# Gated-delta inverse: the transposed factor of the next level by TensorE transposes in place of a second product

## Chip, cores and metric

One core of one Trainium2 chip runs the whole program in one launch. The metric is the device time of one execution in microseconds (us). Names of engines here and in the profile: TensorE is PE (its weight loads PEld), VectorE is DVE, ScalarE is ACT, GpSimd is POOL, SyncE is SP.

## What is computed

The reference is a stack of transformer blocks on 256 tokens of width 1024, in fp32: four blocks of feed-forward, mixer, feed-forward (mixers: gated delta, stick-breaking, sparse attention, gated delta), then a second stack of two blocks. The change lies in the gated-delta mixer (eight heads of 128, chunks of 64 tokens), in the solution of a triangular system for each head and chunk:

```
lower = jnp.where(strict, beta[..., :, None] * kk * decay, 0.0)
eye = jnp.eye(c, dtype=jnp.float32)
rhs = jnp.concatenate([v * beta[..., None], k * (beta * jnp.exp(g_cum))[..., None]], axis=-1)
sol = lax.linalg.triangular_solve(lower + eye, rhs, left_side=True, lower=True, unit_diagonal=True)
```

## The kernel before, in words

The kernel works with tiles of 128 tokens in place of chunks of 64 and inverts the unit triangular matrix itself. A mixer handles its heads in two halves of four heads; with two token tiles each, a half inverts eight 128x128 matrices at once. They form two groups of four, A and B, and a group fills one bank of PSUM (`wrk`, four banks, 128x512 fp32 each).

`invert(half)` doubles the size of the inverted diagonal blocks in six levels (`LEVELS`, block sizes 2 to 64). V is the inverse so far, kept in `g_vi`, and U its transpose, kept in `g_u`; both are parts of `arena`. GpSimd multiplies the transposed matrix with the mask of a level into `g_lts` (two buffers, L2366). For each group a level does:

- X = product of `g_lts` and `g_vi` on TensorE (L848), which ScalarE copies from PSUM to `g_xs` (`copy_out`, the helper at L1124);
- Y = product of `g_u` and `g_xs`, and YT = product of `g_xs` and `g_u` (both L856); VectorE subtracts Y from `g_vi` and YT from `g_u` (both L1949). The last level needs only U, so it makes only YT.

Ahead of level 0 the eight matrices U are transposed on TensorE to give V (L840). Behind the last level `states` multiplies with U (`u0`, L865).

The order is written out by hand. Each engine runs its own program, and semaphores join them: `filled` counts the PSUM banks that TensorE has filled, `taken` those that have been read out. The list `gdn_uses` gives the order in which banks are used, and `taken` rises in that order only: a reader waits, beside its bank, until all uses ahead of it in the list have been taken (`frees`), and TensorE fills a bank only when the use four places back has been taken (`bank`). `held(label)` makes TensorE wait until that use has been taken, since its next product reads what the taker wrote.

After each level VectorE and ScalarE do a job that has nothing to do with the inversion (`jobs(lv)`). In the first half VectorE's are the taps of the convolution at levels 0 to 2 (`taps`, six instructions, L1849), then the low part of a weight piece at levels 3 and 4 (`w_lo`, L1633, 128x2048). In the second half they are weight pieces at levels 0, 1 and 4, and at levels 2 and 3 the gated output of a pair of heads (L1984) and its low part `h_lo` (L1645), which waits for ScalarE's `h_hi` of the same pair; ScalarE makes that in its own job one level later, behind its copies of X. ScalarE's other jobs are weight pieces (`w_hi`), silu and table loads.

Weight pieces of 1 MB come by SyncE's queue into three slots (`raw`); ScalarE makes `w_hi` and VectorE `w_lo` of them, and TensorE multiplies with both.

Of the kernel before, what the change touches and what calls it, by code (L numbers as in the profile page):

```python
# [14 lines left out]
P = 128  # L15
T = 256
# [11 lines left out]
LEVELS = [2, 4, 8, 16, 32, 64]  # L28
# [72 lines left out]
def gdn_uses():  # L101
    u = ["gates", "cols"]
    for half in range(2):
        u += [f"D{half}{p}" for p in range(2)] + [f"ss{half}{p}" for p in range(4)]
        for n in ("kk", "B", "kq"):
            u += [f"{n}{half}{p}" for p in range(2)]
        u += [f"tr{half}{p}" for p in range(3)]
        u += [f"vt{half}{g}" for g in "AB"]
        for lv in range(len(LEVELS)):
            u += [f"X{half}{lv}{g}" for g in "AB"]  # L110
            for g in "AB":
                u += ([f"Y{half}{lv}{g}"] if lv < len(LEVELS) - 1 else []) + [f"YT{half}{lv}{g}"]
        u += [f"u0_{half}", f"S_{half}", f"R_{half}", f"u1_{half}"]
        u += [f"o{half}0", f"o{half}1", f"os{half}0", f"os{half}1"]
    return u
# [153 lines left out]
def build(nc, wts, vec_d, const_d, x_d, c_d, bias_d, mods_d, rows_d, out, ops):  # L269
    starts, use, total = schedule(ops)  # L270

    with ExitStack() as ctx:
# [36 lines left out]
        def cst(name, a=0, b=None):  # L309
            at, w = CONST[name]  # L310
            return const[:, at + a:at + (w if b is None else b)]
# [56 lines left out]
        filled = sem("filled")  # L368
# [160 lines left out]
        def _(pe):  # L529
# [225 lines left out]
            def gdn(i, name, prm):  # L755
# [77 lines left out]
                def invert(half):  # L833

                    k = 2 * g + half
                    pe.wait_ge(stage("gdn_u1"), k + 1)
                    for a, grp in enumerate("AB"):
                        o = put(f"vt{half}{grp}")
                        for b in range(4):
                            m = tr(o[:, b * P:(b + 1) * P], g_u[:, 4 * a + b, :], cst("ident"))  # L840
                        m.then_inc(filled, 1)
                    for lv in range(nl):
                        pe.wait_ge(stage("gdn_lts"), nl * k + lv + 1)
                        for a, grp in enumerate("AB"):
                            o = put(f"X{half}{lv}{grp}")
                            held(f"vt{half}{grp}" if lv == 0 else f"YT{half}{lv - 1}{grp}")
                            for b in range(4):
                                m = mm(o[:, b * P:(b + 1) * P], g_lts[:, lv % 2, 4 * a + b, :], g_vi[:, 4 * a + b, :], start=True, stop=True)  # L848
                            m.then_inc(filled, 1)
                        for a, grp in enumerate("AB"):  # L850
                            held(f"X{half}{lv}{grp}")
                            for label, lh, rh in (("Y", g_u, g_xs), ("YT", g_xs, g_u)):
                                if label == "YT" or lv < nl - 1:
                                    o = put(f"{label}{half}{lv}{grp}")
                                    for b in range(4):
                                        m = mm(o[:, b * P:(b + 1) * P], lh[:, 4 * a + b, :], rh[:, 4 * a + b, :], start=True, stop=True)  # L856
                                    m.then_inc(filled, 1)

                def states(half, between):

                    k, heads = 2 * g + half, range(half * HALF, half * HALF + HALF)
                    held(f"YT{half}{nl - 1}B")
                    o = put(f"u0_{half}")
                    for b in range(HALF):
                        m = mm(o[:, b * P:(b + 1) * P], g_u[:, 2 * b, :], g_bv[:, 2 * b, :], start=True, stop=True)  # L865
                    m.then_inc(filled, 1)
                    between(0)
                    held(f"u0_{half}")
                    o = put(f"S_{half}")
                    for b in range(HALF):  # L870
                        m = mm(o[:, b * P:(b + 1) * P], g_kd[:, b, :], g_u0[:, b, :], start=True, stop=True)
                    m.then_inc(filled, 1)
                    between(1)
                    held(f"S_{half}")
                    o = put(f"R_{half}")
                    for b in range(HALF):
                        m = mm(o[:, b * P:(b + 1) * P], g_k[:, heads[b], P:T], g_s[:, b, :], start=True, stop=True)
                    m.then_inc(filled, 1)
                    between(2)
                    held(f"R_{half}")  # L880
                    o = put(f"u1_{half}")
                    for b in range(HALF):
                        m = mm(o[:, b * P:(b + 1) * P], g_u[:, 2 * b + 1, :], g_bv[:, 2 * b + 1, :], start=True, stop=True)
                    m.then_inc(filled, 1)
                    between(3)
                    held(f"u1_{half}")
                    for j in range(2):
                        o = put(f"o{half}{j}")
                        for b in (2 * j, 2 * j + 1):
                            w = (b % 2) * T  # L890
                            mm(o[:, w:w + P], g_u0[:, b, :], g_qk[:, b, 0:P], start=True, stop=True)
                            mm(o[:, w + P:w + T], g_s[:, b, :], g_q[:, heads[b], P:T], start=True, stop=False)
                            m = mm(o[:, w + P:w + T], g_vi[:, b, :], g_qk[:, b, P:T], start=False, stop=True)
                        m.then_inc(filled, 1)
                    between(4)
                    for j in range(2):
                        pe.wait_ge(stage("gdn_osq"), 2 * k + j + 1)
                        mm(put(f"os{half}{j}"), cst("ones"), g_lts[:, j, 0:4, :].rearrange("p a b -> p (a b)"), start=True, stop=True).then_inc(filled, 1)
                    between(5)
# [726 lines left out]
        def _(dve):  # L1626
# [186 lines left out]
            def gdn(i, name, prm):  # L1813
# [4 lines left out]
                def frees(label):  # L1818
                    dve.wait_ge(taken, use[name, label])
# [119 lines left out]
                def invert(half, jobs):  # L1939

                    for lv in range(len(LEVELS)):
                        for a, grp in enumerate("AB"):
                            for label, t in (("Y", g_vi), ("YT", g_u)):
                                if label == "YT" or lv < len(LEVELS) - 1:
                                    l_ = f"{label}{half}{lv}{grp}"
                                    full(l_)
                                    frees(l_)
                                    v = flat(t[:, 4 * a:4 * a + 4, :])
                                    tt(v, v, bk(l_), ALU.subtract).then_inc(taken, 1)  # L1949
                        jobs(lv)  # L1950

# [681 lines left out]
```

## Time and profile before

| | |
|---|---|
| Median of 3 executions | 3757.82 us (3750.78 to 3761.15) |
| The profiled execution | 3753.37 us |
| Its span in the profile | 3751.3 us |
| PE busy | 3521.9 us, 94% |
| DVE busy | 2192.3 us, 58% |
| ACT busy | 1872.8 us, 50% |
| POOL busy | 583.7 us, 16% |
| Mean granted TensorE clock | 0.971 of full |
| HBM over the span | 173 GB/s |

The profile is one execution. Busy shares are averages over stages with different limits; what counts here is what each engine does within the four inversions, which begin at 326.80, 418.60, 2047.20 and 2138.99 us of the span. An idle time in a row is that of its engine just ahead of the row, with what ended it. A product of two fp32 tiles of 128x128 shows as two rows of TensorE, a transpose as one. A timeline merges rows of one kind that follow each other; a merged row's length runs to the end of its last one, which overlaps the next by the depth of the pipeline. PEclk is the granted clock as a share of 2.4 GHz. A row of windows gives a stretch's start and end, its length, the busy time and instructions of PE, PEld, DVE, ACT and POOL in this order, then PEclk, the busy share of the DMA engines and GB/s.

### The profile page before, as it was taken

What the parts mean: (1) busy time and instruction counts of PE and PEld (TensorE: products, weight loads), DVE (VectorE), ACT (ScalarE), POOL (GpSimd) and SP (SyncE); (2) the same over time, 40 slices, a digit from 0 to 9 for tenths busy, and PEclk for the clock granted to TensorE, in tenths of its full rate; (3) what the DMA queues carried; (4) which work ended last, traced back from release to release, by engine and by line L of the source; (5) the groups of instructions that cost most, each with busy time, mean ns of one, the idle gap of its engine ahead of it and who ended that gap; (6) DMA issues with size and microseconds to landing.
All of it is one profiled execution on the core that took longest, in us unless ns stands there. A gap on an engine that the chain in (4) does not pass through costs nothing. (4 is left out here: it accounts for less than half of the span.)

```text
span 3751.3 us, 44766 instructions
## 1 busy us (share of the span) xinstructions
PE 3521.9 (94%) x18374; PEld 2981.0 (79%) x18374; DVE 2192.3 (58%) x2284; ACT 1872.8 (50%) x2398; POOL 583.7 (16%) x208
## 2 busy tenths in 40 slices
PE   7999899999899997799999999999999799999999
PEld 6889778888788876688878878888888478788887
DVE  4666566665666666666567555555555544545554
ACT  4664356664456562456564444555443344544443
POOL 1511115240134330143421100000000000000000
PEclk9999899999999998899999899999999899999999
DMA  6642156564376753376753135555554125454453
GB/s 247 226 156 78 47 191 224 216 229 161 112 270 241 274 204 122 124 258 254 257 185 112 58 134 190 180 185 185 180 181 165 37 92 187 170 176 160 169 202 129
DMA packets 89975, 653.54 MB, mean 174 GB/s; under 512 B 10032, under 2 KB 10032, under 8 KB 10928
## 3 DMA queue, kind: packets, MB, share of 16 engines
q1 hardware_dynamic: 78768, 573.10, 42.2%
q0 software_dynamic: 11008, 77.60, 5.8%
q8 instruction: 148, 2.42, 0.3%
q14 instruction: 51, 0.42, 0.0%
HBM read 649.61 MB, written 1.05 MB: 173 GB/s over the span
## 5 line engine op out<-in xcount | busy, mean ns | idle before, releaser
L1633 DVE TENSOR_TENSOR w_lo<-raw,w_hi 128x2048 fp32r<-128x2048 f32 x540 | 1391.2, 2581 | 684.2 <-ACT w_hi L1124 684.1
L1124 ACT ACTIVATE w_hi<-raw 128x2048 fp32r<-128x2048 f32 x540 | 1030.3, 1912 | 550.3 <-PE acc L540 376.5
L538 PE MATMUL wrk<-w_hi,h_hi 128*128 128x512 f32 (+1 forms) x2496 | 967.6, 388 | 35.2 <-DVE w_lo L1633 23.2
L540 PE MATMUL wrk<-w_hi,h_lo 128*128 128x512 f32 (+1 forms) x2496 | 952.4, 382 | 0.0
L539 PE MATMUL wrk<-w_lo,h_hi 128*128 128x512 f32 (+1 forms) x2496 | 950.9, 381 | 0.0
L538 PEld LDWEIGHTS wrk<-w_hi,h_hi 128*128 128x128 f32 x2496 | 470.6, 189 | 125.8 <-DVE w_lo L1633 29.6
L2389 POOL TENSOR_TENSOR arena<-arena,c 128x2048 f32<-128x2048 f32 x92 | 467.2, 5082 | 562.1 <-ACT arena L1124 531.5
L540 PEld LDWEIGHTS wrk<-w_hi,h_lo 128*128 128x128 f32 x2496 | 470.4, 188 | 92.0
L539 PEld LDWEIGHTS wrk<-w_lo,h_hi 128*128 128x128 f32 x2496 | 471.0, 189 | 84.5 <-issue 0.2
L538 PE MATMUL acc<-w_hi,hid_hi 128*128 128x512 f32 x1144 | 448.1, 392 | 2.9 <-DVE hid_lo L1713 2.8
L540 PE MATMUL acc<-w_hi,hid_lo 128*128 128x512 f32 x1144 | 445.4, 389 | 0.0
L539 PE MATMUL acc<-w_lo,hid_hi 128*128 128x512 f32 x1144 | 445.1, 389 | 0.0
L1124 ACT ACTIVATE hid_hi<-wrk 128x512 fp32r<-128x512 f32 x143 | 85.5, 598 | 466.8 <-PE wrk L635 466.8
L1124 ACT ACTIVATE arena<-wrk 128x256 f32<-128x256 f32 (+2 forms) x261 | 127.0, 488 | 300.7 <-PE wrk L540 170.6
L538 PEld LDWEIGHTS acc<-w_hi,hid_hi 128*128 128x128 f32 x1144 | 214.7, 188 | 49.1 <-issue 5.7
L540 PEld LDWEIGHTS acc<-w_hi,hid_lo 128*128 128x128 f32 x1144 | 214.7, 188 | 45.1
L539 PEld LDWEIGHTS acc<-w_lo,hid_hi 128*128 128x128 f32 x1144 | 214.9, 188 | 43.7
L1124 ACT ACTIVATE arena<-arena 128x1024 f32<-128x1024 f32 (+2 forms) x238 | 231.5, 979 | 26.8 <-DVE arena L2058 17.5
L538 PE MATMUL wrk<-h_hi,w_hi 128*128 128x256 f32 x660 | 194.6, 295 | 24.7 <-DVE h_lo L1664 14.6
L1713 DVE TENSOR_TENSOR hid_lo<-wrk,hid_hi 128x512 fp32r<-128x512 f32 x143 | 98.3, 687 | 204.0 <-ACT hid_hi L1124 204.0
L539 PE MATMUL wrk<-h_lo,w_hi 128*128 128x256 f32 x660 | 192.7, 292 | 0.0
L540 PE MATMUL wrk<-h_hi,w_lo 128*128 128x256 f32 x660 | 192.4, 292 | 0.0
(267 smaller groups left out, 3887.1 us busy)
## 6 DMA issues: line engine op xcount, KB each, us to landing
raw<-in_wts SPq DMA_DIRECT2D x540, 1024.0 KB, 4.8
arena<-in_mods POOLq DMA_DIRECT2D x72, 1024.0 KB, 5.2
const<-in_const SPq DMA_DIRECT2D x1, 2176.0 KB, 10.2
c<-in_bias POOLq DMA_DIRECT2D x8, 256.0 KB, 3.0
x<-in_x SPq DMA_DIRECT2D x1, 1024.0 KB, 5.3
c<-in_c SPq DMA_DIRECT2D x1, 1024.0 KB, 5.0
out<-x SPq DMA_DIRECT2D x1, 1024.0 KB, 3.9
row<-in_rows SPq DMA_DIRECT2D x1, 512.0 KB, 11.5
```

Of the source, the lines that this page charges most:

```text
L538: nc.tensor.matmul(o, l_h, r_h, start=first, stop=False, skip_group_check=True)
L539: nc.tensor.matmul(o, l_h, r_l, start=False, stop=False, skip_group_check=True)
L540: return nc.tensor.matmul(o, l_l, r_h, start=False, stop=last, skip_group_check=True)
L1124: return nc.scalar.activation(o, i, f, **kw)
L1633: tt(w_lo[:, ns % SLOTS, :], raw[:, ns % SLOTS, :], w_hi[:, ns % SLOTS, :].bitcast(F32), ALU.subtract).then_inc(lo_ready, 1)
L1713: tt(hid_lo[:, s % 2, :, :], wrk[:, use[name, f"t{s}"] % BANKS, :].rearrange("p (a b) -> p a b", b=T), hid_hi[:, s % 2, :, :].bitcast(F32) ...
L2389: nc.gpsimd.tensor_tensor(halves(m_prod[:, g % 2, :]), halves(m_raw[:, m % 2, :]), m_rows[:, w, :].unsqueeze(1).to_broadcast([P, 2, D]), A ...
```

## The change

`YT` as a second product at levels 0 to 4 is gone. In its place TensorE transposes V at the start of the next level (`T`, levels 1 to 5), and VectorE copies the result over U. At level 0 U is still the matrix that V was transposed from. The order of bank uses in a level is now X of A and B, T of A and B, Y of A and B; the last level makes its product with the operands swapped and subtracts it from U, as YT did. `Y` waits for both the X and the T of its group.

```diff
--- before.py
+++ after.py
@@ -107,9 +107,8 @@
         u += [f"tr{half}{p}" for p in range(3)]
         u += [f"vt{half}{g}" for g in "AB"]
         for lv in range(len(LEVELS)):
-            u += [f"X{half}{lv}{g}" for g in "AB"]
-            for g in "AB":
-                u += ([f"Y{half}{lv}{g}"] if lv < len(LEVELS) - 1 else []) + [f"YT{half}{lv}{g}"]
+            for n in ("X", "T", "Y"):
+                u += [f"{n}{half}{lv}{g}" for g in "AB" if n != "T" or lv]
         u += [f"u0_{half}", f"S_{half}", f"R_{half}", f"u1_{half}"]
         u += [f"o{half}0", f"o{half}1", f"os{half}0", f"os{half}1"]
     return u
@@ -843,23 +842,30 @@
                         pe.wait_ge(stage("gdn_lts"), nl * k + lv + 1)
                         for a, grp in enumerate("AB"):
                             o = put(f"X{half}{lv}{grp}")
-                            held(f"vt{half}{grp}" if lv == 0 else f"YT{half}{lv - 1}{grp}")
+                            held(f"Y{half}{lv - 1}{grp}" if lv else f"vt{half}{grp}")
                             for b in range(4):
                                 m = mm(o[:, b * P:(b + 1) * P], g_lts[:, lv % 2, 4 * a + b, :], g_vi[:, 4 * a + b, :], start=True, stop=True)
                             m.then_inc(filled, 1)
+                        if lv:
+                            for a, grp in enumerate("AB"):
+                                o = put(f"T{half}{lv}{grp}")
+                                for b in range(4):
+                                    m = tr(o[:, b * P:(b + 1) * P], g_vi[:, 4 * a + b, :], cst("ident"))
+                                m.then_inc(filled, 1)
                         for a, grp in enumerate("AB"):
                             held(f"X{half}{lv}{grp}")
-                            for label, lh, rh in (("Y", g_u, g_xs), ("YT", g_xs, g_u)):
-                                if label == "YT" or lv < nl - 1:
-                                    o = put(f"{label}{half}{lv}{grp}")
-                                    for b in range(4):
-                                        m = mm(o[:, b * P:(b + 1) * P], lh[:, 4 * a + b, :], rh[:, 4 * a + b, :], start=True, stop=True)
-                                    m.then_inc(filled, 1)
+                            o = put(f"Y{half}{lv}{grp}")
+                            if lv:
+                                held(f"T{half}{lv}{grp}")
+                            lh, rh = (g_u, g_xs) if lv < nl - 1 else (g_xs, g_u)
+                            for b in range(4):
+                                m = mm(o[:, b * P:(b + 1) * P], lh[:, 4 * a + b, :], rh[:, 4 * a + b, :], start=True, stop=True)
+                            m.then_inc(filled, 1)
 
                 def states(half, between):
 
                     k, heads = 2 * g + half, range(half * HALF, half * HALF + HALF)
-                    held(f"YT{half}{nl - 1}B")
+                    held(f"Y{half}{nl - 1}B")
                     o = put(f"u0_{half}")
                     for b in range(HALF):
                         m = mm(o[:, b * P:(b + 1) * P], g_u[:, 2 * b, :], g_bv[:, 2 * b, :], start=True, stop=True)
@@ -1939,13 +1945,16 @@
                 def invert(half, jobs):
 
                     for lv in range(len(LEVELS)):
-                        for a, grp in enumerate("AB"):
-                            for label, t in (("Y", g_vi), ("YT", g_u)):
-                                if label == "YT" or lv < len(LEVELS) - 1:
-                                    l_ = f"{label}{half}{lv}{grp}"
-                                    full(l_)
-                                    frees(l_)
-                                    v = flat(t[:, 4 * a:4 * a + 4, :])
+                        last = lv == len(LEVELS) - 1
+                        for n in ("T", "Y") if lv else ("Y",):
+                            for a, grp in enumerate("AB"):
+                                l_ = f"{n}{half}{lv}{grp}"
+                                full(l_)
+                                frees(l_)
+                                v = flat((g_u if n == "T" or last else g_vi)[:, 4 * a:4 * a + 4, :])
+                                if n == "T":
+                                    nc.vector.tensor_copy(v, bk(l_)).then_inc(taken, 1)
+                                else:
                                     tt(v, v, bk(l_), ALU.subtract).then_inc(taken, 1)
                         jobs(lv)
```

TensorE's program from the transposes ahead of level 0 to the product behind the last level, first half of a mixer, before (L848 is X, L856 is Y and YT, L865 is u0, counts are products; levels 2 to 4 repeat level 1):

```order
L840 MATMUL wrk<-const,arena 128x128 x8
L848 MATMUL wrk<-arena 128x128 x8
L856 MATMUL wrk<-arena 128x128 x16
L848 MATMUL wrk<-arena 128x128 x8
L856 MATMUL wrk<-arena 128x128 x16
...
L848 MATMUL wrk<-arena 128x128 x8
L856 MATMUL wrk<-arena 128x128 x8
L865 MATMUL wrk<-arena 128x128 x4
```

The same place after the change (L847 is X, L853 the transposes T, L862 is Y, L871 is u0; levels 2 to 4 repeat level 1):

```order
L839 MATMUL wrk<-const,arena 128x128 x8
L847 MATMUL wrk<-arena 128x128 x8
L862 MATMUL wrk<-arena 128x128 x8
L847 MATMUL wrk<-arena 128x128 x8
L853 MATMUL wrk<-const,arena 128x128 x8
L862 MATMUL wrk<-arena 128x128 x8
...
L847 MATMUL wrk<-arena 128x128 x8
L853 MATMUL wrk<-const,arena 128x128 x8
L862 MATMUL wrk<-arena 128x128 x8
L871 MATMUL wrk<-arena 128x128 x4
```

Between X and Y there are now eight transposes from level 1 on, eight products follow where sixteen did, and the last level has a row more.

VectorE's program in the first half, levels 0 to 1, before (L1949 are the takes, L1849 the taps of the job):

```order
L1949 TENSOR_TENSOR arena<-arena,wrk 128x512 x4
L1849 SCALAR_TENSOR_TENSOR arena<-acc,vec,arena 128x255 x2
L1849 SCALAR_TENSOR_TENSOR arena<-acc,vec,arena 128x254 x2
L1849 SCALAR_TENSOR_TENSOR arena<-acc,vec,arena 128x253 x2
L1949 TENSOR_TENSOR arena<-arena,wrk 128x512 x4
L1849 SCALAR_TENSOR_TENSOR c<-acc,vec,c 128x255 x2
L1849 SCALAR_TENSOR_TENSOR c<-acc,vec,c 128x254 x2
L1849 SCALAR_TENSOR_TENSOR c<-acc,vec,c 128x253 x2
```

and after the change (L1956 the copies of T, L1958 the subtractions, L1855 the taps):

```order
L1958 TENSOR_TENSOR arena<-arena,wrk 128x512 x2
L1855 SCALAR_TENSOR_TENSOR arena<-acc,vec,arena 128x255 x2
L1855 SCALAR_TENSOR_TENSOR arena<-acc,vec,arena 128x254 x2
L1855 SCALAR_TENSOR_TENSOR arena<-acc,vec,arena 128x253 x2
L1956 COPY arena<-wrk 128x512 x2
L1958 TENSOR_TENSOR arena<-arena,wrk 128x512 x2
L1855 SCALAR_TENSOR_TENSOR c<-acc,vec,c 128x255 x2
L1855 SCALAR_TENSOR_TENSOR c<-acc,vec,c 128x254 x2
L1855 SCALAR_TENSOR_TENSOR c<-acc,vec,c 128x253 x2
```

Level 0 has two takes in place of four; from level 1 on two copies stand ahead of two subtractions, and the job comes behind all four as it did.

## Rows read from the trace of the kernel before

**Rows 1.** Windows over the two inversions of the first mixer.
```profile
326.80:359.38 32.58, 31.80 (x272) 30.90 (x272) 26.81 (x42) 18.25 (x21) 9.52 (x4) 1.00 0.12 35
418.60:455.52 36.92, 34.27 (x272) 33.18 (x273) 26.00 (x33) 14.64 (x21) 13.14 (x5) 0.94 0.19 61
```

**Rows 2.** TensorE timeline, first half: start us, length us, work, [idle before <- releaser].
```profile
326.80 2.02 PE L848 MATMUL wrk<-arena 128*128 128x128 f32 x16 [0.64 <-ACT arena L1124]
...
328.66 3.79 PE L856 MATMUL wrk<-arena 128*128 128x128 f32 x32
...
332.29 2.17 PE L848 MATMUL wrk<-arena 128*128 128x128 f32 x16
...
337.87 2.17 PE L848 MATMUL wrk<-arena 128*128 128x128 f32 x16
...
354.59 2.17 PE L848 MATMUL wrk<-arena 128*128 128x128 f32 x16
...
359.38 1.16 PE L865 MATMUL wrk<-arena 128*128 128x128 f32 x8 [0.78 <-DVE arena L1949]
```

**Rows 3.** VectorE timeline, first half.
```profile
329.81 0.69 DVE L1949 TENSOR_TENSOR arena<-arena,wrk 128x512 f32<-128x512 f32 x1 [8.20 <-PE wrk L856]
...
332.49 0.69 DVE L1949 TENSOR_TENSOR arena<-arena,wrk 128x512 f32<-128x512 f32 x1 [0.21 <-PE wrk L856]
...
333.09 2.68 DVE L1849 SCALAR_TENSOR_TENSOR arena<-acc,vec,arena 128x255 f32<-128x255 f32 x6
...
335.69 3.07 DVE L1949 TENSOR_TENSOR arena<-arena,wrk 128x512 f32<-128x512 f32 x4
...
355.40 2.28 DVE L1633 TENSOR_TENSOR w_lo<-raw,w_hi 128x2048 fp32r<-128x2048 f32 x1
```

**Rows 4.** ScalarE timeline, first half: copy of X, group A, level 2.
```profile
338.96 0.60 ACT L1124 ACTIVATE arena<-wrk 128x512 f32<-128x512 f32 x1 [2.07 <-PE wrk L848]
```

**Rows 5.** TensorE timeline: the eight transposes before the first half's level 0.
```profile
325.13 1.03 PE L840 MATMUL wrk<-const,arena 128*128 128x128 f32 x8
```

**Rows 6.** Instructions of L1968: engine, form, count: shortest/median/longest ns.
```profile
L1968 DVE COPY c<-wrk x8: 690/692/692, 376.1 to 2188.9; 128x512 f32<-128x512 f32 x8
```

**Rows 7.** TensorE timeline, second half.
```profile
418.60 3.78 PE L848 MATMUL wrk<-arena 128*128 128x128 f32 x16 [0.71 <-POOL arena L2366]
...
422.17 4.28 PE L856 MATMUL wrk<-arena 128*128 128x128 f32 x32
...
437.44 2.16 PE L848 MATMUL wrk<-arena 128*128 128x128 f32 x16
...
444.20 1.13 PE L848 MATMUL wrk<-arena 128*128 128x128 f32 x8 [1.03 <-DVE arena L1949]
...
445.79 1.13 PE L848 MATMUL wrk<-arena 128*128 128x128 f32 x8 [0.45 <-DVE arena L1949]
...
450.32 1.06 PE L848 MATMUL wrk<-arena 128*128 128x128 f32 x8
...
455.52 1.16 PE L865 MATMUL wrk<-arena 128*128 128x128 f32 x8 [0.78 <-DVE arena L1949]
```

**Rows 8.** VectorE timeline, second half.
```profile
423.81 0.69 DVE L1949 TENSOR_TENSOR arena<-arena,wrk 128x512 f32<-128x512 f32 x1 [7.70 <-PE wrk L856]
...
440.57 2.10 DVE L1645 TENSOR_TENSOR h_lo<-h,h_hi 128x256 fp32r<-128x256 f32 x2 [1.45 <-ACT h_hi L1124]
...
442.59 3.04 DVE L1949 TENSOR_TENSOR arena<-arena,wrk 128x512 f32<-128x512 f32 x4
...
447.88 0.76 DVE L1645 TENSOR_TENSOR h_lo<-h,h_hi 128x256 fp32r<-128x256 f32 x2 [1.45 <-ACT h_hi L1124]
```

**Rows 9.** Windows over two stretches of the stick-breaking mixer, columns as in rows 1.
```profile
972.90:986.50 13.60, 7.93 (x42) 6.36 (x41) 9.44 (x22) 6.99 (x17) 0.00 (x0) 1.00 0.00 1
986.50:993.30 6.80, 5.68 (x15) 4.43 (x15) 3.11 (x8) 1.48 (x4) 0.00 (x0) 0.50 0.00 0
```

**Rows 10.** GpSimd timeline, first half.
```profile
328.90 2.38 POOL L2366 TENSOR_TENSOR arena<-arena,const 128x1024 f32<-128x1024 f32 x1 [2.46 <-PE wrk L848]
```

## The prediction

> **What bounds the kernel now.** I read the windows over the four inversions first, then each engine's timeline inside them. In the window of an inversion TensorE's records cover 31.80 of 32.58 us in the first half of a mixer and 34.27 of 36.92 in the second, so TensorE looks like the limit [rows 1]. There are four inversions: two gated-delta mixers, two halves each; the second mixer's windows (2047.20 and 2138.99) are as long as the first's. Together they are 139 us of the 3751.3 us span; nothing else is edited.
>
> The timeline of TensorE shows the period. Levels begin at 326.80, 332.29 and 337.87, and the last at 354.59 [rows 2]: levels 1 to 4 take 22.30 / 4 = 5.58 us each. A level is 48 rows (each fp32 product of 128x128 shows as two rows): 16 of X (L848), 32 of Y and YT (L856). From 328.66 to 332.29 there are 32 rows, 3.63 us, 0.112 per row beside a slower first one, so 48 rows are 5.4 us; the other 0.2 us is group B of X waiting for the last subtraction. VectorE is nearly as full: four subtractions and a job of six tap instructions follow each other without a gap, 333.09 to 335.69 and 3.07 us on [rows 3]. So two engines bind at once, and removing TensorE work is worth only what the second one and the chain between them leave.
>
> The chain has these hops. From the first row of a group of eight to the start of its reader: 337.87 to 338.96, 1.09 us, on ScalarE [rows 2, 4]; 328.66 to 329.81, 1.15 us, on VectorE [rows 2, 3]. From the end of a VectorE take to TensorE's next row: four takes end at 442.59 + 3.04 = 445.63 and TensorE resumes at 445.79, 0.16 us [rows 7, 8]. Takes that wait for each other start 0.79 us apart (3.04 to 3.07 for four, 0.69 each); an unrelated job starts 0.60 us after the last take (332.49 to 333.09) [rows 3].
>
> **What the change removes and adds.** Per inversion the second product (YT) goes from levels 0 to 4: 40 products, 80 rows. The last level keeps the one product per head that it had, and levels 1 to 5 get eight transposes each, 40 rows. A transpose is one row: eight at L840 take 1.03 us with the last row's own length of about 0.27 in it, so 0.109 apiece [rows 5]. Counted: before 96 + 88 x 2 = 272 rows, which is the count in the window [rows 1]; after 96 + 96 + 40 = 232. Forty rows less at 0.112 is 4.5 us per inversion, 18 us in all. That is the most the change can give, reached if no new wait appears.
>
> VectorE's work hardly changes: a level keeps four takes, two being copies instead of subtractions. The nearest row for such a copy is COPY c<-wrk of 128x512, 0.69 us, the same as a subtraction (0.69) [rows 3, 6]. Level 0 has two takes fewer, the last level two more. ScalarE and GpSimd issue what they did; no DMA moves, and each queue past the takes (pieces to split, taps) follows the same level as before.
>
> What changes is the order of waiting. Before, both products of a level start from X, and the next X may start while the YT subtraction runs. Now one level is a serial loop: X, ScalarE's copies of X, the copy of T (which the order of takes puts behind both X copies), Y, subtraction, next X.
>
> **Cost level by level** (first half, full clock). I count from the start of the first T copy. It ends at 0.69; Y of group A starts at 0.85, its subtraction at 2.0 (hop 1.15), that of B 0.90 later at 2.9; VectorE's job starts at 3.5.
> - Levels 1 to 3, job of taps 2.60 (333.09 to 335.69 [rows 3]): the next T copy starts at 6.05 to 6.10. I take 6.05 against 5.58: +0.47 each, +1.4.
> - Level 4, job one weight piece, 2.28 [rows 3]: 5.7 against 5.58, +0.1. Without any job the other loop closes at: X of B at 0.90, its copy at 1.98 to 2.58, T copy 2.68 to 3.37, Y at 3.53, subtraction 4.64 to 5.33, X at 5.5. So even an idle VectorE gives no gain.
> - Level 0: two X groups 1.86 (326.80 to 328.66), 1.15 to the subtraction, 0.69, 0.16: 3.9 against 5.49 [rows 2]: -1.6. This is the one real saving.
> - Last level: T copy at 2.8, Y of A at 3.65, Y of B at 4.54, its subtraction 5.65 to 6.34, next stage at 6.5. Before it is 354.59 to 359.38, 4.79 [rows 2]: +1.7.
>
> First half: -1.6 + 1.4 + 0.1 + 1.7 = **+1.6**.
>
> Second half. Level 0 starts at half clock (418.60 to 422.17 for 16 rows, 0.22 per row [rows 7]); the subtraction comes at 423.81 [rows 8], X again 0.69 + 0.16 later: 6.1 against 7.69 (level 3 starts at 437.44, two levels of 5.58 earlier level 1 at 426.29), -1.6. Levels 1 and 2 carry a weight piece: +0.1 each. At level 3 VectorE is blocked in its job till 442.59, 5.15 into the level: its h_lo waits for ScalarE's h_hi and stands beside GpSimd's multiply [rows 7, 8]. Before, two subtractions then release X (444.20, 6.76). Now copy 0.69, hop 0.16, Y and hop 1.11, subtraction 0.69, hop 0.16 give about 7.9: +1.1. Level 4 the same way: h_lo ends at 448.64 [rows 8], 2.85 after group B of X at 445.79, which now starts 0.9 into the level; VectorE is free at 3.7, the same 2.8 follow, 6.5 against 6.12: +0.4. Last level 6.5 against 5.20: +1.3. Sum **+1.4**.
>
> All: 2 x (1.6 + 1.4) = **+6 us**. Nothing behind gives it back: the stage after an inversion starts with the product that waits for its last take (359.38, 0.78 idle before it [rows 2]), and TensorE is the busy engine from there on. The hops are the soft spot: like ones differ by 0.06 among themselves (1.09, 1.15) and a level has four, so 0.2 us per level, over 22 levels 4.4 us either way.
>
> Against which time: the profiled execution took 3753.37, the median of the three others is 3757.82, and they spread over 10.4 us (3750.78 to 3761.15). The middle of all four is 3755.6; with +6 I say **3761.6**. A difference under 0.3%, 11.3 us, is what a measurement of this kernel cannot tell from none; +6 lies inside.
>
> **A rule against the change.** The granted clock is 1.00 in the first half's inversion and 0.94 in the second's, which begins at the lower level [rows 1, 7]. In the new loop with taps X and T fill the first 2.7 us of a level and Y begins at about 4.05, so TensorE stands still for 1.4 us of each 6.05, beside 0.87 of transposes. In the trace a thinner feed, 7.93 busy of 13.60 us, ran at 1.00, though the clock was 0.50 right after it [rows 9]. So I expect the clock to stay.
> The Trainium skill, in "TensorE: Matmul & The Clock Gate", Part 4 (PE-mode transpose), says that transposes do not count as activity of TensorE in the way products do; by that rule the transposes would be as good as idle and the clock could fall in every inversion. The trace does not decide it: no stretch before alternates products and transposes like this.
>
> **The rivals.**
> - *Slower, by the clock.* If TensorE falls to 1.2 GHz once in each inversion for 6.8 us (the length of 986.5 to 993.3, a stretch at 0.50 [rows 9]), each fall costs about 3: four falls add 12, +18 in all, 3773. If it stays low throughout, each level is some 2 us longer (groups of eight rows 1.7 instead of 0.9 [rows 7], part of it beside VectorE), +45, 3800. It decides from two inversions on. For it: the idle time; against: the 7.93 of 13.60. Chance 0.06.
> - *Slower, by the copies.* h_lo took 2.10 us for two when GpSimd multiplied, 0.76 when it did not [rows 8]. GpSimd's multiply starts when X of B is full, and the T copies fall into it at levels 1 to 3. If they stretch by 1.3 us as h_lo did, it is 12 x 1.3 = 16 more, +22, 3777. Against: the subtraction at 329.81 took its 0.69 beside the multiply of 328.90 to 331.28 [rows 3, 10]; like the copy it reads PSUM. Chance 0.05.
> - *Faster, TensorE alone binds.* If the takes come earlier than I count and only rows matter, -18, 3738. For it: the busy share in the windows [rows 1]. Against: the taps fill VectorE. It needs over 11 of the 18 us; chance 0.04.
> - *The loop is as I say, the hops are shorter or the last level cheaper*: 0 to +3, 3756 to 3759, inside no change.
>
> **How the numbers follow.** The forecast with its short-hop variant has 0.85, all of it within 0.3% but for a tail: +6 with 4.4 of hops and some 5 us of spread between executions passes +11.3 in perhaps one case in sixteen. That gives faster 0.04, same 0.81, slower 0.15. The range takes 4.4 and 5 us plus about 4 for where the runs lie downwards, 3748, and reaches up to the cheaper of the slower rivals, 3776.
>
> **What would show it.** In the changed profile: levels of the first half 6.05 us at levels 1 to 3, 5.7 at level 4, 3.9 at level 0, 6.5 at the last; window of a first half 34.2 us, of a second 38.3; 232 TensorE rows in each; TensorE idle about 1.4 us before L862 in each level, released by the COPY at L1956; that COPY 0.69 us also beside GpSimd; granted clock 1.00 in the first halves. Wrong it would be with the level at 5.0 us or less, the copy well below 0.69, or half clock inside an inversion.

## The result and the profile after

| | before | after |
|---|---|---|
| Median of 20 executions each | 3751.28 us (3747.40 to 3761.15) | 3757.05 us (3752.51 to 3765.83) |
| The profiled execution, its span | 3753.37, 3751.3 us | 3761.97, 3760.2 us |
| PE busy | 3521.9 us, 94% | 3509.9 us, 93% |
| DVE, ACT, POOL busy | 2192.3, 1872.8, 583.7 us | 2191.5, 1876.6, 586.7 us |
| Mean granted clock | 0.971 | 0.971 |

The ratio after to before is 1.0016, with a 95% interval of 1.0009 to 1.0022: 6.0 us slower on 3751.28 (the medians differ by 5.8), and less than the 0.3% that the prediction set as its bound of no change. TensorE has 12 us less to do and the kernel is a little longer. The ratios here and below leave out two executions that ran slow, one of e11 (8734 us at a granted clock of 0.401) and one of the kernel before beside it (4036 us at 0.835).

The windows of the changed kernel, columns as in [rows 1]: first inversion, the stage between, second inversion, for mixer 1 and then mixer 2.

```profile
328.61:362.93 34.32, 28.36 (x233) 26.44 (x233) 26.69 (x42) 18.53 (x21) 9.47 (x4) 1.00 0.16 56
362.93:421.37 58.44, 51.19 (x329) 44.91 (x329) 25.12 (x43) 22.02 (x29) 2.40 (x2) 0.89 0.12 41
421.37:461.06 39.69, 31.59 (x232) 29.79 (x232) 25.84 (x33) 14.83 (x22) 13.10 (x5) 0.91 0.22 74
2050.63:2084.94 34.31, 28.36 (x232) 26.43 (x232) 26.70 (x42) 18.53 (x21) 9.48 (x4) 1.00 0.17 54
2084.94:2144.17 59.23, 52.02 (x328) 45.74 (x329) 25.12 (x43) 22.20 (x29) 2.41 (x2) 0.87 0.11 41
2144.17:2182.51 38.34, 30.63 (x232) 28.70 (x232) 25.75 (x33) 14.66 (x21) 13.10 (x5) 0.94 0.23 77
```

The three stretches of mixer 2 before, and the stage of mixer 1:

```profile
359.38:418.60 59.22, 52.12 (x329) 45.84 (x329) 25.11 (x43) 22.42 (x30) 2.42 (x2) 0.87 0.14 53
...
2047.20:2079.78 32.58, 31.80 (x272) 30.91 (x273) 26.82 (x42) 18.25 (x21) 9.51 (x4) 1.00 0.11 36
2079.78:2138.99 59.21, 52.13 (x328) 45.85 (x328) 25.11 (x43) 22.42 (x30) 2.41 (x2) 0.87 0.15 53
2138.99:2175.88 36.89, 34.25 (x273) 33.15 (x273) 25.98 (x33) 14.64 (x21) 13.14 (x5) 0.94 0.19 61
```

The four inversions took 138.97 us before and take 146.66 after, 7.7 more. TensorE has 232 rows in each where it had 272, and is busy 28.36 of 34.32 us where it was busy 31.80 of 32.58: the rows that went became idle time. The stages between a mixer's two inversions are together 0.8 us shorter. The spans of the two profiles differ by 8.9 us, so 2.0 lie in neither.

TensorE's timeline in the first half, levels 0 to 2 and the end, answers to [rows 2]:

```profile
328.61 2.02 PE L847 MATMUL wrk<-arena 128*128 128x128 f32 x16 [0.64 <-ACT arena L1130]
330.47 2.01 PE L862 MATMUL wrk<-arena 128*128 128x128 f32 x16
332.46 2.02 PE L847 MATMUL wrk<-arena 128*128 128x128 f32 x16
334.32 1.04 PE L853 MATMUL wrk<-const,arena 128*128 128x128 f32 x8
336.55 2.02 PE L862 MATMUL wrk<-arena 128*128 128x128 f32 x16 [1.19 <-DVE arena L1956]
338.55 2.02 PE L847 MATMUL wrk<-arena 128*128 128x128 f32 x16
...
354.43 2.02 PE L862 MATMUL wrk<-arena 128*128 128x128 f32 x16 [0.80 <-DVE arena L1956]
356.43 2.02 PE L847 MATMUL wrk<-arena 128*128 128x128 f32 x16
...
360.12 2.02 PE L862 MATMUL wrk<-arena 128*128 128x128 f32 x16 [0.80 <-DVE arena L1956]
362.93 1.16 PE L871 MATMUL wrk<-arena 128*128 128x128 f32 x8 [0.78 <-DVE arena L1958]
```

Level 0 takes 332.46 - 328.61 = 3.85 us, level 1 338.55 - 332.46 = 6.09 (levels 2 and 3 the same), level 4 5.70 and the last 362.93 - 356.43 = 6.50. In each level from 1 on TensorE has nothing to do ahead of L862 until VectorE's first copy ends (335.72 + 0.69 = 336.41 in the rows below; L862 starts 0.14 later). VectorE there, answering to [rows 3]:

```profile
333.12 2.68 DVE L1855 SCALAR_TENSOR_TENSOR arena<-acc,vec,arena 128x255 f32<-128x255 f32 x6
335.72 1.47 DVE L1956 COPY arena<-wrk 128x512 f32<-128x512 f32 x2
337.72 0.69 DVE L1958 TENSOR_TENSOR arena<-arena,wrk 128x512 f32<-128x512 f32 x1 [0.52 <-PE wrk L862]
338.61 0.69 DVE L1958 TENSOR_TENSOR arena<-arena,wrk 128x512 f32<-128x512 f32 x1 [0.20 <-PE wrk L862]
```

The transposes ended at 335.36, but VectorE is in its taps until 335.8. Only then does it copy, and it waits 0.52 us for the product that waited for its copy. Both engines wait in turn in the same level.

The instructions of L1956 (shortest/median/longest ns) with who waited for them, and those of L862 with what they waited for:

```profile
L1956 DVE COPY arena<-wrk x40: 678/691/693, 335.7 to 2179.7; 128x512 f32<-128x512 f32 x40
who waited for it (us, times):
  PEld wrk L862: 28.8, 20
  PE wrk L862: 24.6, 20
```

```profile
L862 PE MATMUL wrk<-arena x384: 274/275/422, 330.5 to 2181.5; 128*128 128x128 f32 x192
its engine sat idle before it (us, times) until:
  DVE arena L1956: 53.4, 40
```

The 53.4 us are the waits of the weight loads (28.8) and of the products (24.6) of the same 20 places, so TensorE's products stood still for 24.6 us for those copies. In the second half the longest wait is the one that the prediction placed at level 3; TensorE's rows there:

```profile
440.68 1.04 PE L853 MATMUL wrk<-const,arena 128*128 128x128 f32 x8
444.64 2.73 PE L862 MATMUL wrk<-arena 128*128 128x128 f32 x16 [2.93 <-DVE arena L1956]
447.17 2.91 PE L847 MATMUL wrk<-arena 128*128 128x128 f32 x16
449.92 1.04 PE L853 MATMUL wrk<-const,arena 128*128 128x128 f32 x8
452.56 2.02 PE L862 MATMUL wrk<-arena 128*128 128x128 f32 x16 [1.61 <-DVE arena L1956]
```

and the clock behind it:

```profile
445.80:449.20 3.40, 3.40 (x18) 3.40 (x18) 2.17 (x4) 0.08 (x1) 0.00 (x0) 0.50 0.02 5
```

Behind 2.93 us without work, sixteen rows take 2.73 and 2.91 us in place of 2.02: the clock was at its lower level, 1.2 GHz, from 445.8 to 449.2. The same wait in mixer 2 had no such stretch. There level 3 took 7.83 us and level 4 6.50, where mixer 1 has 8.35 and 7.39: the stretch cost about 1.4 us.

### The profile page after: what moved, and what is told of

Read it like the earlier page. It is cut to its first block and busy times, and to the rows that moved or that the text cites. A ratio compares the mean times of both kernels' runs of the same rounds, so it can differ in the third digit from the quotient of the medians.

```text
span 3760.2 us, 44446 instructions
## 1 busy us (share of the span) xinstructions
PE 3509.9 (93%) x18214; PEld 2964.3 (79%) x18214; DVE 2191.5 (58%) x2284; ACT 1876.6 (50%) x2398; POOL 586.7 (16%) x208
## 3 DMA queue, kind: packets, MB, share of 16 engines
q8 instruction: 147, 2.41, 0.3%
```

## The experiments

Levels are told from the start of X to the next start of X, the last one to u0 (L865, L871). "Windows" are first inversion, stage, second inversion, in mixer 1, then in mixer 2. Each of the windows comes from one profiled execution, each ratio from timed ones beside executions of the kernel before on the same chip.

### Which engine copies: e1_copies_on_scalar

```diff
 ScalarE, invert, against after.py
-                        for a, grp in enumerate("AB"):
-                            copy_out(f"X{half}{lv}{grp}", g_xs[:, 4 * a:4 * a + 4, :])
+                        for n in ("X", "T") if lv else ("X",):
+                            for a, grp in enumerate("AB"):
+                                copy_out(f"{n}{half}{lv}{grp}", (g_xs if n == "X" else g_u)[:, 4 * a:4 * a + 4, :])
 VectorE, invert (cut: the rest of the loop, which keeps Y alone)
-                        for n in ("T", "Y") if lv else ("Y",):
-                            for a, grp in enumerate("AB"):
-                                l_ = f"{n}{half}{lv}{grp}"
+                        for a, grp in enumerate("AB"):
+                            l_ = f"Y{half}{lv}{grp}"
```

> The changed kernel with the copies of T on ScalarE, behind its copies of X; order of banks kept. Theory (serial loop, stretched where VectorE's job delays the T copy: levels 6.09, 5.70 us in the changed kernel's trace): the T copy starts 2.68 us into a level whatever VectorE's job is, and takes ScalarE's 0.60, so X follows at about 5.4; first half 32.2 instead of 34.3 us, second 36.2 instead of 38.3, 8 us under the changed kernel and 2 under the one before (ratio to before 0.9994). Rival (ScalarE's own jobs, 1.9 us, and table loads delay the X copies as much as VectorE's did T): no gain on the changed kernel, ratio 1.0016.

Measured: 3748.97 us against 3753.64, ratio 0.9988 (0.9980 to 0.9997). Windows 32.40, 59.23, 35.52 and 32.40, 59.22, 35.20. TensorE's timeline:

```profile
332.16 2.02 PE L847 MATMUL wrk<-arena 128*128 128x128 f32 x16
334.02 1.04 PE L853 MATMUL wrk<-const,arena 128*128 128x128 f32 x8
335.65 2.02 PE L862 MATMUL wrk<-arena 128*128 128x128 f32 x16 [0.59 <-ACT arena L1130]
337.65 2.02 PE L847 MATMUL wrk<-arena 128*128 128x128 f32 x16
```

A tap level is 5.49 us where it was 6.09, and the wait 0.59 where it was 1.19. Nothing is computed otherwise; the copy only no longer stands behind VectorE's job. So the copy behind the taps was the term that made these levels longer. The serial loop of the prediction is still there, at about the 5.5 us that it had for a level "without any job".

### The order of the banks: e2_transposes_first

The order in a level is T and X of group A, T and X of group B, then Y of A and of B. ScalarE makes the copies of both T and X, as in e1.

```diff
 gdn_uses, against e1
-            for n in ("X", "T", "Y"):
-                u += [f"{n}{half}{lv}{g}" for g in "AB" if n != "T" or lv]
+            for g in "AB":
+                u += [f"T{half}{lv}{g}"] * (lv > 0) + [f"X{half}{lv}{g}"]
+            u += [f"Y{half}{lv}{g}" for g in "AB"]
 TensorE and ScalarE: the same order in their loops (cut)
```

> T copies on ScalarE, and the order of banks in a level is T, X of group A, T, X of group B, Y of A and B. Theory (the loop, not TensorE's 40 rows of 0.112 us, sets the level): Y of A may start when X of B is done, subtraction at 3.8 to 4.5, next level at 4.6 us, which is also TensorE's own 40 rows; 5.6 where ScalarE loads a table or VectorE stands in its h_lo. First half about 28.9 us, second about 34.2; 13 us under the kernel before, ratio 0.9966. Rival (the levels have another floor, such as VectorE's jobs or the weight stream behind the inversion taking the gain back): ratio 0.999 to 1.000, with TensorE waiting longer in the stages behind.

Measured: 3735.93 us, ratio 0.9958 (0.9946 to 0.9971). Windows 29.24, 58.57, 33.75 and 29.25, 53.97, 33.08.

```profile
331.69 0.63 PE L849 MATMUL wrk<-const,arena 128*128 128x128 f32 x4
332.15 1.06 PE L855 MATMUL wrk<-arena 128*128 128x128 f32 x8
333.05 0.60 PE L849 MATMUL wrk<-const,arena 128*128 128x128 f32 x4
333.48 1.06 PE L855 MATMUL wrk<-arena 128*128 128x128 f32 x8
334.38 2.06 PE L864 MATMUL wrk<-arena 128*128 128x128 f32 x16
336.31 0.63 PE L849 MATMUL wrk<-const,arena 128*128 128x128 f32 x4
```

336.31 - 331.69 = 4.62 us for 40 rows, without one idle time: here TensorE binds, and the 40 rows fewer are worth what the count said (5.58 - 4.62 = 0.96, for eight rows 0.9). The gain was in the change all along, locked up by the order of takes and by the engine of the copy. Not all of the 0.42% is the loop's: in the profiles the four inversions are 13.7 us shorter (125.32 against 138.97) and the stages 5.9, which e8 below looks into, while 1.6 us come back elsewhere. The new order with the copies left on VectorE was not run, so the share of the order alone is not known.

### Level 0 alone: e3_level0_only

This is the kernel before, but without YT at level 0 and with transposes at level 1 only.

```diff
 gdn_uses, against before.py
+            u += [f"T{half}{lv}{g}" for g in "AB"] * (lv == 1)
             for g in "AB":
-                u += (...) + [f"YT{half}{lv}{g}"]
+                u += (...) + [f"YT{half}{lv}{g}"] * (lv > 0)
 TensorE and VectorE: the same in their loops (cut)
```

> The kernel before with the change at level 0 alone: no YT at level 0, T transposed and copied at level 1, YT kept at levels 1 to 4. Theory (the saving of level 0 is real, 1.6 us, but the next level pays for it since its products wait for the T copy): level 0 3.85, level 1 about 7.6 us with taps and 7.3 with a weight piece instead of 5.58; sum +0.3 per inversion, about +1 us in all, ratio 0.9995 to 1.001. Rival (level 0 can be had by itself): -1.6 x 4 = -6.5 us, ratio 0.9983.

Measured: 3743.83 us against 3753.76, ratio 0.9978 (0.9970 to 0.9987). The inversions did what was expected: 33.04, 36.60, 33.04 and 36.48, sum 139.16 against 138.97; level 0 is 3.85 and level 1, with six takes, 7.67. The total did not: it is 8.3 us shorter by the ratio and 9.9 by the medians. The difference lies in the stages behind the first inversions, 10.5 us less in the profile:

```profile
361.18:415.13 53.95, 46.30 (x328) 40.84 (x328) 25.11 (x43) 22.23 (x30) 2.40 (x2) 0.96 0.15 57
...
2074.89:2128.85 53.96, 46.32 (x328) 40.85 (x328) 25.11 (x43) 22.24 (x30) 2.40 (x2) 0.96 0.15 57
```

The same 328 rows took 59.2 us before, with a mean granted clock of 0.87 where it is 0.96 here. No instruction of that stage was touched. This raised the question of e8 to e11.

### Are the rows really hidden: e4_transposes_twice, e5_identity_products

e4 issues each transpose of the changed kernel twice, with the same result; e5 makes T as a product with the identity, two rows in place of one.

```diff
 e4, TensorE, T of after.py
-                                for b in range(4):
+                                for b in (0, 1, 2, 3) * 2:
 e5
-                                    m = tr(o[:, b * P:(b + 1) * P], g_vi[:, 4 * a + b, :], cst("ident"))
+                                    m = mm(o[:, b * P:(b + 1) * P], g_vi[:, 4 * a + b, :], cst("ident"), start=True, stop=True)
```

> The changed kernel with each transpose issued twice into the same place: 40 rows more per inversion, 0.109 us each, 4.4 us. Theory (TensorE waits 1.19 us for the T copy in levels with taps and 0.80 in the others): the rows fall into that wait, about +0.1 us in 2 levels of 5, under 2 us in all, ratio to before 1.0016 to 1.0021. Rival (TensorE's rows bound the inversion): 4 x 4.4 = +17 us on the changed kernel, ratio 1.006. If transposes count as work for the granted clock, the fall to half clock that the changed kernel shows once, in the second half of the first mixer, is gone.

> The changed kernel with each transpose made as a product with the identity, two rows each instead of one: same number of rows as with every transpose twice, but products. Theory: the same time as that one, ratio to before 1.0016 to 1.0021, TensorE's wait for the T copy shorter by 0.87 us. If transposes are as good as idle for the clock and that cost the changed kernel something, this one has no fall to half clock inside an inversion and is 1 to 2 us faster than the one with every transpose twice; rival: both the same.

Measured: e4 3758.14 us, ratio 1.0012 (1.0003 to 1.0021); e5 3756.99, ratio 1.0014 (1.0005 to 1.0023). First inversions take 34.45 and 34.49 us, against 34.31 in after, with all the 40 rows back: 0.14 us for 4.4 us of TensorE. The rows alone don't set the time.

The granted clock at level 3 of the second half, e5 in both mixers and then e4 in mixer 2:

```profile
440.50:443.90 3.40, 3.40 (x19) 3.40 (x18) 1.34 (x3) 0.00 (x0) 0.00 (x0) 0.50 0.00 0
2160.80:2164.20 3.40, 3.40 (x18) 3.40 (x18) 1.28 (x3) 0.00 (x0) 0.00 (x0) 0.50 0.00 0
```

```profile
2162.80:2166.20 3.40, 3.40 (x18) 3.40 (x17) 1.30 (x3) 0.00 (x0) 0.00 (x0) 0.50 0.00 0
```

With products in place of transposes the stretch at 1.2 GHz came in two of two mixers, with transposes in one of two each (after, e4, and e11 below, whose sixteen rows behind the wait took 3.41 us in mixer 1 and 2.02 in mixer 2). These kernels reach the wait at different moments, since the stage ahead of it was 59.2 us long in e4's mixer 1, without a stretch, and 55.6 in the three others of e4 and e5, with one. So e5 against e4 doesn't tell transposes from products. All first inversions, with eight or sixteen transposes in each level from 1 on, stayed at 1.00.

### The best order with h_lo a level later: e6_h_lo_a_level_later, e7_h_lo_alone, e12_after_h_lo_later

At level 3 of the second half VectorE's `h_lo` waits for an `h_hi` that ScalarE makes later in the same level. All three move `h_lo` by one level, to e2 (e6), to before (e7) and to after (e12).

```diff
 VectorE, jobs of the second half
                         gated(0, lv - 2)
-                        lowered(2 * (lv - 2))
+                        if lv == 3:
+                            lowered(0)
                     elif lv == 4:
+                        lowered(2)
                         piece(18)
```

> The kernel with the transposes first and T copied on ScalarE, and in the second half VectorE's h_lo moved one level later (behind the subtractions of levels 3 and 4), so that it no longer stands in h_lo while ScalarE and GpSimd work. Theory (VectorE's wait in its job delays the subtraction of levels 3 and 4 of the second half): these levels fall to about 5 and 4.6 us, 1.2 to 2.7 us per second half, 3 to 5 us less than with the transposes first alone, ratio to before 0.9945 to 0.995. Rival (h_lo is hidden): same as without it, 0.9958.

> The kernel before with the move of h_lo alone. Levels 3 and 4 of the second half take 6.76 and 6.12 us in it instead of 5.58, and the last 5.20 instead of 4.79; theory: 1.2 + 0.5 us per second half, 3 us in all, ratio 0.9992, less where h_lo at level 4 now stands in the way of the last takes. Rival: no difference, 1.0000.

> The changed kernel with VectorE's h_lo in the second half moved behind the subtractions of levels 3 and 4. In the changed kernel these levels take 7.82 and 6.51 us (without a fall of the clock), TensorE idle 2.93 and 1.61 us for the T copy that stands behind h_lo. Theory: both at about 5.7 us or a little less, 2.1 + 0.8 us per second half, -5.8 us in all and no half clock inside an inversion, ratio to before 1.0000. Rival (h_lo moved only shifts the wait to the next level): 1.0016 as the changed kernel.

| | ratio | second inversions | level 3, level 4, last (mixer 1) |
|---|---|---|---|
| before | 1 | 36.92, 36.89 | 6.76, 6.12, 5.20 |
| e7 | 0.9996 (0.9987 to 1.0004) | 35.29, 35.16 | 5.57, 5.58, 5.21 |
| after | 1.0016 (1.0009 to 1.0022) | 39.69, 38.34 | 8.35, 7.39, 6.50 |
| e12 | 0.9984 (0.9975 to 0.9992) | 35.82, 35.56 | 5.60, 5.59, 7.17 |
| e2 | 0.9958 (0.9946 to 0.9971) | 33.75, 33.08 | 6.65, 5.66, 5.06 |
| e6 | **0.9937 (0.9923 to 0.9950)** | 31.14, 31.21 | 4.93, 4.97, 5.21 |

In each kernel the step saves inside the inversion; to after it gives most (3.9 and 2.8 us), since there the late copy held up a whole serial level, and it takes the stretch at 1.2 GHz away. Part of the wait moved into the last level there, 7.17 us for 6.50. e7 saved 1.7 us per inversion and nothing that its ratio could tell from none. The totals of e6 and e12 fell by more than was expected (0.9937 for 0.9945 to 0.995, 0.9984 for 1.0000). For e12 the profile shows 3.6 us of that in the stages (58.53 and 55.56 against 58.44 and 59.23 in after), which the step does not touch. e6, 3729.81 us against 3753.76, beats both kernels.

### A little work more: e8_two_products_more, e9_six_products_more, e10_e6_two_more, e11_after_ten_more

The question of e3: does the stage behind the first inversion depend on when the inversion ends? Each of these repeats the last product of group B at the last level of the first half: twice more (e8, on before), six times (e9, on before), twice (e10, on e6), ten times (e11, on after). The value is the same.

```diff
 e8, TensorE, invert, against before.py
-                                    for b in range(4):
+                                    for b in [0, 1, 2, 3] + [3] * (2 if half == 0 and lv == nl - 1 and grp == "B" else 0):
```

> The kernel before with two products repeated (0.45 us of TensorE) at the end of each mixer's first inversion, nothing else. The profiles so far show the stage between the two inversions of a mixer at 59.2 us with 15.8 at half clock (before, both mixers), at 53.97 with 4 (change at level 0 alone, whose first inversion is 0.46 us longer), 55.6 and 58.5 in others. Theory (the inversions' length shifts this stage against the moments at which the granted clock may change, and a shift of half a microsecond spares the stage a stretch at half clock): stage 53.97 in both mixers, 2 x (0.45 - 5.25) = -9.6 us, ratio 0.9975. Rival (the short stage came from something in the other kernel): +0.9 us, ratio 1.0002.

> The same with six products repeated, 1.34 us, close to the 1.73 us by which the change lengthens a first inversion. Theory of the shift: the stage behind at 58.5 us as in the changed kernel's first mixer, 2 x (1.34 - 0.7) = +1.3 us, ratio 1.0002 to 1.0005, clearly slower than with two. Rival (no effect of the shift): +2.7 us, 1.0007, and the one with two at 1.0002.

> The fastest so far (transposes first, h_lo a level later) with the same two products repeated. Its profile has one such stage at 53.97 and one at 59.22 us. Theory of the shift: both at 53.97, +0.9 - 5.2 = -4.3 us, near 3725, ratio 0.9925. Rival: +0.9 us on 0.9937.

> The changed kernel with ten products repeated at the end of each first inversion, 2.23 us each. Theory of the shift: the stage behind falls from 58.4 and 59.2 to 53.97 us, 2 x 2.23 - 4.5 - 5.2 = -5 us on the changed kernel in spite of 4.5 us of added work, ratio to before about 1.000. Rival: +4.5 us on the changed kernel, ratio 1.0028.

| | time | ratio | first inversions | stages |
|---|---|---|---|---|
| e8 | 3743.41 | 0.9975 (0.9965 to 0.9984) | 33.03, 33.03 | 53.99, 54.00 |
| e9 | 3752.24 | 0.9998 (0.9989 to 1.0007) | 33.93, 33.92 | 58.40, 55.33 |
| e10 | 3728.44 | 0.9936 (0.9924 to 0.9949) | 29.69, 29.70 | 53.99, 53.98 |
| e11 | 3755.72 | 1.0009 (1.0000 to 1.0018) | 36.55, 36.54 | 53.98, 53.98 |

(Before, beside these: 3751.49 us.) e8 adds 0.45 us of work twice and is 8.1 us faster by the medians, 9.4 by the ratio. e9's profile is of its fastest execution (3746.04 us), so its 55.33 need not be usual; its ratio can't be told from none, nor from the expected 1.0002 to 1.0005. The clock of e8, and then that of before, over the same stretch of the span:

```profile
396.00:409.70 13.70, 10.12 (x76) 9.30 (x76) 11.99 (x24) 3.08 (x4) 0.00 (x0) 1.00 0.00 0
410.00:416.80 6.80, 4.67 (x20) 4.27 (x21) 1.57 (x2) 1.79 (x3) 4.68 (x2) 0.50 0.01 2
```

```profile
396.00:409.70 13.70, 12.75 (x49) 11.32 (x50) 6.99 (x10) 1.74 (x1) 0.00 (x0) 0.50 0.00 0
416.50:423.30 6.80, 6.09 (x29) 5.69 (x28) 0.00 (x0) 2.68 (x5) 5.20 (x3) 0.50 0.01 2
```

Before, TensorE runs at 1.2 GHz from 396.0 to 409.7; e8 runs the same stretch at 2.4 GHz and does 76 rows in it where before does 49. Just ahead of it the feed is thin in both. These rows are of the kernel before, the first at full clock with 3.96 us busy of 5.00:

```profile
390.00:395.00 5.00, 3.96 (x27) 3.28 (x26) 0.46 (x1) 4.72 (x7) 0.00 (x0) 1.00 0.00 0
395.00:400.00 5.00, 3.05 (x14) 3.05 (x15) 3.73 (x4) 2.74 (x3) 0.00 (x0) 0.60 0.00 0
```

In e8 the five us from 395.11 hold only 2.41 us of work, and the clock stays up:

```profile
395.11:400.11 5.00, 2.41 (x18) 2.27 (x19) 4.51 (x5) 3.37 (x4) 0.00 (x0) 1.00 0.00 0
```

So a thin feed by itself doesn't bring the fall. One other reading of e8 is that the added products keep TensorE busier ahead of the stage. e3 speaks against it: its first inversions last as long (33.04 us, for 33.03 in e8) with eight rows fewer than before, and its stages are the same 54.0.

e11 is the control for the changed kernel: 2.23 us of work more per first half, 4.5 in all, and it is no slower than after itself (1.0009 against 1.0016). In its profile both stages are at 54.0, 9.7 us less than in after's. e10 is a miss: both its stages are short, as expected, where e6 had 53.97 and 59.22, but the total stayed at e6's. In the profiles its six windows are together 4.4 us shorter than e6's (229.66 against 234.02) and its span only 0.8 (3729.0 against 3729.8): 3.6 us came back outside the windows, 2.4 ahead of the first inversion, 0.2 between the mixers and 1.0 behind. Both profiles are of the slowest of five executions, so e6's others may have had short stages already. Which of the two it was stays open.

## Why the prediction was right, and where it was not

**The sum.** The forecast was +6 us, measured +6.0 by the ratio and +5.8 by the medians. The prediction's absolute 3761.6 stood on a middle of four executions, 3755.6; twenty put before at 3751.28, so after came out at 3757.05, inside the range.

**What bounds.** Two engines and the chain between them, not TensorE alone: shown. e4 put the 40 rows back for 0.14 us; e1 moved the copy, rows unchanged, and got 0.6 us per tap level; e2 changed the order, and only then the count of rows decided.

**First half, level by level.** Level 0 3.9, measured 3.85. Levels 1 to 3 6.05, measured 6.09. Level 4 5.7, measured 5.70. Last 6.5, measured 6.50. Sum +1.6, measured 34.31 - 32.58 = +1.73. The wait ahead of L862 was given as about 1.4 in each level. It is 1.19 behind taps, since X and T fill 2.90 us of the level with the last row's own length and not 2.7, and 0.80 behind a weight piece, where VectorE's job is shorter; the levels hold all the same.

**Second half.** Window 38.3, measured 38.34 in mixer 2, +1.45 for a forecast of +1.4. By level there: 6.11 (6.1), 5.71, 5.69 (+0.1 each), 7.83 (7.9), 6.50 (6.5), 6.50 (6.5). In mixer 1 levels 0 and 1 take 5.67 and 6.09: level 0 ends earlier, and in level 1 VectorE's first copy waits 0.30 us for ScalarE. Together they are the same 11.8 us. VectorE's blocked job at level 3 was the place, as said.

**Prices.** The copy from PSUM takes 0.69 us, also beside GpSimd's multiply, as the prediction had it: 678 to 693 ns over all 40, so the rival of stretched copies is out.

**The clock: the step that was too short.** "So I expect the clock to stay" held in the first halves, not in one of two second halves: 2.93 us without work at level 3 were followed by 3.4 us at 1.2 GHz, which cost about 1.4 us. The prediction had costed that wait but looked for the clock's risk in the 1.4-us waits of every level; the rival's price was "about 3" a fall, for a stretch of 6.8 us and not of 3.4. The Trainium skill, in "TensorE: Matmul & The Clock Gate", Part 4 (PE-mode transpose), has transposes not count as activity like products. Nothing here speaks for that as a cause: the fall came with products too (e5, twice), and 40 transposes ran at 1.00 in every first inversion. Nor is the rule refuted, since the longest idle time in those is 1.19 us.

**"Nothing behind gives it back": wrong as a rule.** The product behind the inversion does wait for its last take, as said (0.78 us idle ahead of L871). But the stage as a whole isn't a fixed length that the delay is added to. It is 54.0, 55.3 to 55.6, 58.4 to 58.6 or 59.2 us, by how long its clock is low, and 0.45 us of added work took it from 59.2 to 54.0 (e8). In the changed kernel it happened to be 58.44 and 59.23 against 59.22 and 59.21, so the omission was worth 0.8 us in that profile. A forecast to within 0.1 us per level could as well have ended 10 us off, on the faster side, as e3's did. So the agreement in the total is in part luck. How much of the +6.0 of the timed executions is such a share stays open: the four inversions gained 7.7 us in the profiles (6.3 without the one fall), and only these were forecast.

## What to carry to other kernels

Before counting an operation that goes, draw the loop of takes and jobs that its replacement stands in: moving one copy off the engine with the job, and taking the transposes first, turned the same 40 rows fewer from +0.16% into -0.42%, and into -0.63% with the late `h_lo` mended. In the four inversions alone that is +7.7, -13.7 and -18.1 us; the rest of each difference is what the stages and other stretches gave or took. Where a stage behind the edit has thin stretches in which the clock falls, a difference of some 0.2% may come from how the edit shifts it in time, so compare the windows of the edited place themselves, and time a control that only shifts (a product repeated) beside the edit.

## What the runs showed of the hardware

A stage of 328 TensorE rows, never edited, took 53.95 to 59.23 us; by the granted clock of its window (0.96 to 0.99 for the short ones, 0.93, 0.89 and 0.87 for the longer), about twice the missing share of its length ran at 1.2 GHz: 2 x 0.13 x 59.2 = 15 us at 0.87, 2 x 0.04 x 54 = 4 at 0.96. The 11 us more at the lower clock go with 5.2 us more of length, so by this estimate each cost about half of itself. Two mixers of one execution can differ (e4 59.21 and 55.56, e6 53.97 and 59.22). The Trainium skill, in "TensorE: Matmul & The Clock Gate", Part 1 (The HAM clock gate), says that the chip looks at TensorE's activity in windows that run on by themselves and don't start with the kernel, and that the number of slow products varies from run to run. That fits mixers that differ behind the same inversion (after 58.44 and 59.23, e12 58.53 and 55.56); it does not by itself explain why e8's nine executions lie within 3.1 us (3742.55 to 3745.60), where the twenty of before spread over 13.8. e3, e8 and e11 show that edits ahead of a stage alone change its clock. By what rule they do stays open, and so does why the added 0.45 us is so steadily good.
